# Small experts' scatter of the rows ahead moved to mid-panel, and TensorE's variants of the expert in another order

## The reference, cut to what matters

```python
def swiglu(h, w1, w3, w2):
    return (jax.nn.silu(h @ w1) * (h @ w3)) @ w2

def expert_block(args):           # within moe_swiglu
    toks, e = args
    xb = xf[toks]
    return (jax.nn.silu(xb @ w1[e]) * (xb @ w3[e])) @ w2[e]
...
y = jnp.zeros((n_tok, d), jnp.float32).at[row_tok].add(out.reshape(n_rows, d).astype(jnp.float32) * row_w[:, None])
```

## Time and profile before

| | us |
|---|---|
| median of 3 runs | 1699.87 (1699.73 to 1705.61) |
| the profiled execution, device time | 1696.55 |
| its span, first to last instruction | 1694.7 |
| TensorE busy | 1528.6 (90%) |
| VectorE busy | 762.5 (45%) |
| ScalarE busy | 510.7 (30%) |
| DMA, mean over the span | 296 GB/s |

### The profile page before, as it was taken

One profiled execution on the slowest core, in us unless ns is written; L12 is line 12 of the kernel. 1 busy time (PEld: TensorE's weight loads), 2 busy tenths in 40 slices (PEclk: granted clock), 3 DMA queues, 4 the chain that ended last, 5 costly groups with the idle time before them and its releaser, 6 DMA issues.

```text
span 1694.7 us, 22256 instructions
## 1 busy us (share of the span) xinstructions
PE 1528.6 (90%) x8462; PEld 1069.9 (63%) x8463; DVE 762.5 (45%) x851; ACT 510.7 (30%) x531; POOL 36.7 (2%) x40
## 2 busy tenths in 40 slices
PE   5999999999999999778999879999787978999974
PEld 2587767888587775334886339999543434788431
DVE  5696777775697675003884001000100100787104
ACT  1375425344275422003773000000100101775000
POOL 1200010000100000000000000000000000000000
PEclk9999999999999999999999999999899999999998
DMA  9885349874497532998998998777499999999994
GB/s 362 307 322 205 124 174 335 283 271 154 145 353 242 180 139 103 395 396 290 393 376 291 394 396 307 262 260 263 147 393 397 392 394 395 367 383 344 362 395 166
DMA packets 210536, 502.36 MB, mean 296 GB/s; under 512 B 9137, under 2 KB 13409, under 8 KB 210481
## 3 DMA queue, kind: packets, MB, share of 16 engines
q1 hardware_dynamic: 208770, 496.15, 80.4%
q0 software_dynamic: 1712, 5.43, 1.0%
HBM read 500.50 MB, written 1.05 MB: 296 GB/s over the span
## 4 chain that ended last, share of the span: by engine, by line
PE 69%; DMA 21%; DVE 5%; issue 2%; ACT 1%; SPq 1%; DVEq 0%; ACTq 0%
DMA w_raw<-in_exp_w_dram 20%; PE ps L1541 12%; PE ps L1542 11%; PE ps L1543 11%; PE ps L2246 6%; PE ps L2188 5%; PE ps L2178 4%; PE ps L1547 4%; PE ps L2256 3%; PE ps L2007 2%; PE ps L1981 2%; PE ps L2108 1%; DMA w_raw<-in_w_mod_mix_dram 1%; SPq L407 1%; DVE gates L1145 1%
## 5 line engine op out<-in xcount | busy, mean ns | idle before, releaser
L2178 PE MATMUL ps<-w_raw,x_rows 128*64 128x256 f32 x2240 | 270.0, 386 | 72.3 <-DMA w_raw<-in_exp_w_dram 60.2
L1541 PE MATMUL ps<-w_hi,actT_hi 128*128 128x512 f32 (+1 forms) x768 | 302.3, 394 | 11.8 <-ACT gates L680 3.5
L1543 PE MATMUL ps<-w_hi,actT_lo 128*128 128x512 f32 (+1 forms) x768 | 294.6, 384 | 0.0
L1542 PE MATMUL ps<-w_lo,actT_hi 128*128 128x512 f32 (+1 forms) x768 | 294.5, 383 | 0.0
L2178 PEld LDWEIGHTS ps<-w_raw,x_rows 128*64 128x64 f32 x2240 | 151.6, 137 | 192.3 <-DMA w_raw<-in_exp_w_dram 106.7
L928 DVE TENSOR_TENSOR w_lo<-w_raw,w_hi 128x2048 fp32r<-128x2048 f32 x78 | 178.5, 2289 | 92.9 <-ACT w_hi L515 92.7
L1443 DVE TENSOR_TENSOR gated<-silu,ps 128x256 f32<-128x256 f32 x35 | 14.7, 421 | 417.4 <-PE ps L2178 417.4
L515 ACT CAST w_hi<-w_raw 128x2048 fp32r<-128x2048 f32 x78 | 148.8, 1909 | 112.1 <-PE ps L1543 97.4
L1344 DVE TENSOR_TENSOR w_lo<-w_raw,w_hi 128x2048 fp32r<-128x2048 f32 x72 | 164.9, 2291 | 26.2 <-ACT w_hi L766 24.0
L1541 PEld LDWEIGHTS ps<-w_hi,actT_hi 128*128 128x128 f32 x768 | 145.8, 190 | 45.5 <-issue 11.9
L1543 PEld LDWEIGHTS ps<-w_hi,actT_lo 128*128 128x128 f32 x768 | 145.6, 190 | 28.8
(11 more groups left out here) (285 smaller groups left out, 1346.2 us busy)
## 6 DMA issues: line engine op xcount, KB each, us to landing
w_raw<-in_exp_w_dram SPq DMA_DIRECT2D x336, 1024.0 KB, 10.9
w_raw<-in_ffn_w_dram SPq DMA_DIRECT2D x33, 1024.0 KB, 5.2
w_raw<-in_w_mod_mix_dram SPq DMA_DIRECT2D x24, 1024.0 KB, 9.1
w_raw<-in_w_mod_ffn_dram SPq DMA_DIRECT2D x24, 1024.0 KB, 5.9
w_raw<-in_w_gate_dram SPq DMA_DIRECT2D x24, 1024.0 KB, 7.0
w_raw<-in_w_in_dram SPq DMA_DIRECT2D x14, 1024.0 KB, 6.6
w_raw<-in_w_out_dram SPq DMA_DIRECT2D x8, 1024.0 KB, 5.0
w_raw<-in_w_branch_c_dram SPq DMA_DIRECT2D x4, 1024.0 KB, 5.0
```

The lines of the kernel that those rows point to most:

```text
L1541: MM(to, hi, w_h, start=first, stop=False)
L1542: MM(to, hi, w_l, start=False, stop=False)
L1543: return MM(to, lo, w_h, start=False, stop=last)
L2178: ins = MM(half(to, c, HALF_N), x_few[:, k, :], w_raw[:, i % RING, at:at + HALF_N], start=k == 0, stop=k == KD - 1)
```

## The change

In the small variant the scatter of the expert ahead, the adds, the turn of the place, its copy and the next picks leave the first panel and stand behind the last piece of the third panel of the panel loop (`LATE`), in PSUM banks 1, 2, 3, 6 (`FEW_SUMS`) and 7 (`FEW_PLACE`), since bank 0 accumulates by then. Bank 0 is opened after a wait for the last expert's results to have been read out of it, and the wait for the new place stands behind the panel loop. DVE's panel loop ends a panel earlier, and the last panel is written out. The scatter of the other variants and the last one behind the loop keep their places; `scatter` waits in addition for the adds of the expert before. TensorE's variants stand in the order two-block, wide, split, small.

```diff
 HALF_N = BANK // 2
 WIDE = P + 16
 LOGITS = 4
+
+LATE = 3
+FEW_SUMS, FEW_PLACE = (1, 2, 3, 6), 7
 
 DVE_MIX_STEPS, DVE_DENSE_STEPS, DVE_ROUTE_STEPS = 39, 22, 32
 ACT_MIX_STEPS = 2
...
                     first_rows(1)
+                    act.sem_inc(y_act, 1)
...
                             act.sem_inc(split_hi, EXPERT.n_split)
                             act.sem_inc(part_hi_ready, 1)
                             gate_of(1, done0, panel_0)
-                            act.wait_ge(place_sent, e + 1)
-                            A(place[:, 0, :], ps[:, 0, 0:SEQ], ACT.Copy).then_inc(place_ready, 1)
                             with act.Fori(1, NP) as p:
                                 done, at = act.snap(done0 + (p - 1) * PANEL_PIECES), act.snap(panel_0 + p)
                                 gate_of(5, done, at)
                                 gT_part(at)
+                                with act.If(p == LATE):
+                                    act.wait_ge(place_sent, e + 1)
+                                    A(place[:, 0, :], ps[:, FEW_PLACE, 0:SEQ], ACT.Copy).then_inc(place_ready, 1)
                             gT_part(panel_0 + NP)
                             with act.If(e < EXPERTS - 1):
                                 first_rows(e + 2)
...
                         dve.wait_ge(gathered_lo[0], n)
                         nc.vector.tensor_copy(x_wide[:, 3:6, :], rows_bank(HW3 + 2)).then_inc(xg_lo_ready[0], 1)
 
-                    def add_rows(experts):
+                    def add_rows(experts, sums=range(4)):
                         for t in range(TT):
                             for c in range(2):
                                 dve.wait_ge(scattered, experts * 4 + (2 * t + c + 1))
                                 part = yacc[:, t, c * BANK:(c + 1) * BANK]
-                                TTn(part, part, bank(2 * t + c), ALU.add).then_inc(added, 1)
+                                TTn(part, part, bank(sums[2 * t + c]), ALU.add).then_inc(added, 1)
 
                     pick_tokens(0)
                     first_rows(1)
+                    dve.sem_inc(y_dve, 1)
                     dve.wait_ge(yacc_zero, 1)
                     with nc.Fori(0, EXPERTS, engines=[dve.engine], hint_back_edge=True, head_slot={dve.engine: 0}) as e:
                         count = dve.value_load(counts_i[0:1, bass.ds(e, 1)], min_val=0, max_val=SEQ)
...
                             dve.sem_inc(gT_lo_ready, NP)
                             dve.sem_inc(ahead_ready, SPLIT)
                             dve.sem_inc(part_lo_ready, 1)
-                            met(0, done0)
-                            met(1, done0)
-                            with dve.If(e > 0):
-                                add_rows(e)
-                            nc.vector.memset(hbuf[HALF_P:P, 0, :], 0.0)
-                            met(2, done0)
+                            for i in range(3):
+                                met(i, done0)
                             gate_of(3, done0, panel_0)
-                            pick_tokens(e + 1)
-                            with dve.Fori(1, NP) as p:
-                                done, at = dve.snap(done0 + (p - 1) * PANEL_PIECES), dve.snap(panel_0 + p)
+
+                            def panel(done, at):
+
                                 for i in (4, 5, 6):
                                     met(i, done)
                                 gate_of(7, done, at)
                                 for i in (8, 9):
                                     met(i, done)
+
+                            with dve.Fori(1, NP - 1) as p:
+                                panel(dve.snap(done0 + (p - 1) * PANEL_PIECES), dve.snap(panel_0 + p))
+                                with dve.If(p == LATE):
+                                    with dve.If(e > 0):
+                                        add_rows(e, FEW_SUMS)
+                                    nc.vector.memset(hbuf[HALF_P:P, 0, :], 0.0)
+                                    dve.wait_ge(place_sent, e + 1)
+                                    pick_tokens(e + 1)
+                            panel(dve.snap(done0 + (NP - 2) * PANEL_PIECES), panel_0 + (NP - 1))
                             done6 = dve.snap(done0 + (NP - 2) * PANEL_PIECES)
 
                             with dve.If(e < EXPERTS - 1):
...
                                     ins = MM(to, part[:, t, k * P:(k + 1) * P], pick[:, t, P:2 * P], start=t == 0, stop=t == 1)
                             ins.then_inc(signal, 1)
 
-                    def scatter(blocks, experts):
-                        pe.wait_ge(y_act, experts)
-                        pe.wait_ge(y_dve, experts)
+                    def scatter(blocks, experts, to):
+                        pe.wait_ge(added, experts * 4)
+                        pe.wait_ge(y_act, experts + 1)
+                        pe.wait_ge(y_dve, experts + 1)
                         for t in range(TT):
                             for c in range(2):
                                 for b in range(blocks):
-                                    ins = MM(bank(2 * t + c), place[:, b, t * P:(t + 1) * P], hbuf[:, b, c * BANK:(c + 1) * BANK],
+                                    ins = MM(bank(to[2 * t + c]), place[:, b, t * P:(t + 1) * P], hbuf[:, b, c * BANK:(c + 1) * BANK],
                                              start=b == 0, stop=b == blocks - 1)
                                 ins.then_inc(scattered, 1)
 
-                    def scatter_rows(experts):
+                    def scatter_rows(experts, to=range(4)):
                         rows_before = nc.snap(rows_reg, min_val=0, max_val=SEQ)
                         with pe.If(rows_before <= P):
-                            scatter(1, experts)
+                            scatter(1, experts, to)
                         with pe.Else():
-                            scatter(2, experts)
+                            scatter(2, experts, to)
 
                     pe.wait_ge(zeros_set, 1)
                     pe.wait_ge(pick_ready, 1)
...
                                     ins = TR(ps[:, HW1, c * P:(c + 1) * P], gated[0][:, c * P:(c + 1) * P], ident)
                                 ins.then_inc(gT_sent, 1)
 
-                            up_raw(0, "A", 0, loads0)
-                            up_raw(1, "A", 1, loads0)
-                            with pe.If(e > 0):
-                                scatter_rows(e)
-                            up_raw(2, "B", 0, loads0)
-                            pe.wait_ge(added, e * 4 + 4)
-                            for t in range(TT):
-                                ins = TR(ps[:, 0, t * P:(t + 1) * P], pick_w[:, t, 0:P], ident)
-                            ins.then_inc(place_sent, 1)
-                            up_raw(3, "B", 1, loads0)
-                            pe.wait_ge(place_ready, e + 1)
+                            for i, kind, h in ((0, "A", 0), (1, "A", 1), (2, "B", 0), (3, "B", 1)):
+                                up_raw(i, kind, h, loads0)
+                            pe.wait_ge(y_act, e + 1)
+                            pe.wait_ge(y_dve, e + 1)
                             MM(bank(0), zeros[:, 0:P], zeros[:, :], start=True, stop=False)
-                            with pe.Fori(1, NP) as p:
-                                loads, at = pe.snap(loads0 + (p - 1) * 16), pe.snap(panel_0 + p)
+
+                            def panel(loads, at):
+
                                 pe.wait_ge(silu_ready, at)
                                 up_raw(4, "A", 0, loads)
                                 up_raw(5, "A", 1, loads)
...
                                 pe.wait_ge(gT_hi_ready, at)
                                 down_raw(8, 0, loads)
                                 down_raw(9, 1, loads)
+
+                            with pe.Fori(1, NP) as p:
+                                panel(pe.snap(loads0 + (p - 1) * 16), pe.snap(panel_0 + p))
+                                with pe.If(p == LATE):
+                                    with pe.If(e > 0):
+                                        scatter_rows(e, FEW_SUMS)
+                                    for t in range(TT):
+                                        ins = TR(ps[:, FEW_PLACE, t * P:(t + 1) * P], pick_w[:, t, 0:P], ident)
+                                    ins.then_inc(place_sent, 1)
+                            pe.wait_ge(place_ready, e + 1)
                             turn(panel_0 + NP)
                             next_rows(1)
                             pe.wait_ge(gT_hi_ready, panel_0 + NP)
...
                                 ins = TR(ps[:, d // 4, d % 4 * P:(d % 4 + 1) * P], yT_whole[:, d, :], ident)
                             ins.then_inc(y_turned, 1)
 
-                        with pe.If(count <= P):
+                        with pe.If(count > WIDE):
+                            gather_second()
+                            expert(2)
+                        with pe.Else():
```

(15 more changed lines are left out.)

## The result

| | before | changed |
|---|---|---|
| median, us | 1702.74 (1699.73 to 1705.86, 4 runs) | 1782.80 (1780.46 to 1785.75, 4 runs) |
| ratio to before | | 1.0485, 95% interval 1.0459 to 1.0511 |
| profiled execution, us | 1696.55 | 1782.34 |
| its span, us | 1694.7 | 1780.4 |

The account below looks back on a forecast made before the run. Bound: weights' DMA in small experts, TensorE in the wide one, both full in split ones (engines taken). Scatter -8, code loads +56.6 and cold clock +9.8 made +58.4 us, forecast median 1758, range 1690 to 1785.

Parts of the forecast that it names:

- the sum of the gaps: TensorE's waits for code at the starts of the eight experts, each entry paying for its far jumps: +56.6 us.
- E5's term: Start of a small expert after a small one: six landed pieces wait for TensorE, which catches up; 0, at most +6 us.
- the price of a load: TensorE's fetch of code not held: 3.1 us with the weights' DMA idle, 5.3 with it full.
- the loop's end before E2 and E7: Jump to the loop's end before two small experts: paid as before at the first, 1.3 us added at the second.
- E4's term: Start of the small expert after the wide one: two more loads at 3.1 us, +6.2.
- E0: First expert in the loop, a small one: its entry pays three loads at 3.1 us, +9.3.
- E6: Seventh expert in the loop, a split one: its entry pays two loads at 5.3 us, +10.6.
- The scatter, -8: Scatter moved to mid-panel in small experts: saves DMA idle time at their starts, -8 us, bounds 0 and -15.4.
- The cold clock, +9.8: First pieces run slower behind new long gaps before four experts: 1.95, 2.9, 2.9 and 1.95 us.
- Rival 1: TensorE keeps the loop's code held, only the first expert's loads are paid: -8.4 us, 1691; chance 0.24.
- Rival 3: Mid-panel scatter in small experts becomes a DVE wait delaying slot releases: +12 us, 1712 if alone; chance 0.04.
- The rule of the Trainium skill's page: Only two code lines held, so jumps back to the loop's head cost some 22 us more, about 1780; weighed, not adopted.

Follow-up runs that it names:

- order alone: Kernel before with TensorE's variants in the order of the change, the scatter left where it was: 1791.69 us, ratio 1.0527 to before.
- scatter alone: Changed kernel with TensorE's dispatch put back as before (small variant first), so only the scatter moves to mid-panel: 1689.05 us, ratio 0.9937 to before.
- the kernel without the two-block code: Changed kernel minus TensorE's code for the two-block variant, never run on this input; variant order otherwise kept, small one last: 1686.33 us, ratio 0.9912 to before.
- wide last: Kernel before with the mid-panel scatter and the two large variants swapped in memory (small, split, two-block, wide): 1686.13 us, ratio 0.9942 to before.
- Large first, then small and split: Mid-panel scatter, memory order two-block, wide, small, split, compare for the large ones at the loop's head: 1702.79 us, ratio 1.0039 to before.

## Why the prediction was right and wrong

The forecast was slower by 58 us, by code fetched again at every entry, in a range of 1690 to 1785; measured were 1782.80 and 82 us by the ratio. The mechanism is the one forecast: the run with the order alone has the whole loss and its gaps, the run with the scatter alone has a gain. The step that failed is the sum of the gaps, put at +56.6 us: they measured +83.8, or 78.6 after what E5 won back. Three of its parts were too low, namely E5's term (0, with 10.1 left of 15.3), the price of a load (3.1, where a jump took 4.25 to 4.6) and the loop's end before E2 and E7 (1.3, where a fourth jump was paid in full). E4's term erred the other way, by 10.8, so that part of the nearness of 1758 to 1783 is luck. Gaps in detail, forecast and measured in the two profiles:

| entry | forecast | measured |
|---|---|---|
| E0 | +9.3 | 13.49 - 0.72 = +12.8 |
| E1 | +5.3 | 12.68 - 5.29 = +7.4 |
| E2 | +9.3 | 17.78 - 1.26 = +16.5 |
| E3 | +5.3 | +5.5 |
| E4 | +6.2 | 4.81 - 9.41 = -4.6 |
| E5 | 0 | +15.3, of which 10.1 stayed |
| E6 | +10.6 | +12.7 |
| E7 | +10.6 | +18.3 |

- **The price of a load, 3.1 us, was too low.** I divided E4's gap of 9.41 by its three packets. A jump is what is paid, not a packet: with the DMA idle 4.25 us each at E0, and the dispatch of the change makes three of them. With the DMA full one jump took 4.9 to 5.5 us (4.92, 5.20, 5.41 and 5.47 above), as forecast for E3; the two before E1 and E6 took 12.68 and 12.65, 6.3 each where 5.3 was forecast.
- **E2 and E7** are reached from the split variant, which no longer runs into the loop's end: by the order of the code four jumps to code not held stand in a row (to the end, the second compare, the third, the small variant), 17.78 and 18.33, 4.4 to 4.6 each. I counted three and 1.3 for the end, because that was its visible remnant at E2 before.
- **E4 had the wrong sign.** After the wide expert I had all of the small one's way loaded again. By the order of the code the head and the compares had just been used by the wide expert or stand next to it, so that only the small variant's own packets were missing. The gap of 4.81 us, the price of one jump, fits that.
- **E5's zero was wrong**, the largest single error of reasoning. I let six landed pieces wait for TensorE. A stage bound by bytes has no store of landed pieces: E4's last ones were used as they came, and behind them only those already asked for could arrive. The strip above shows what that is worth: the DMA is full for some 9 us of the gap of 15.32 and empty for some 10, and E5, which takes 106.6 us after its gap where it took 111.8 before (start to start less the gap at E6, 119.2 - 12.65), wins back 5.2; in the run with the scatter alone, where E5 has no gap, it takes 111.8 as before. The rest, 10.1, is lost.
- **The scatter, -8**, measured -10.7 (7.5 to 13.8) alone and some -7 by the ratios of the change and the order alone. By stretch of the two profiles E4 gave 4.6 (forecast 4.2), E7 1.7 (1.5), and E2 0.5 in place of 2.2, for which no run gives the reason. No cost of the mid-panel place shows.
- **The cold clock, +9.8**: outside the gaps the stretches of the changed kernel differ from before by +1.1 (E0), -0.9, +1.3, +4.8, -4.6, -5.2, +1.4 and +1.1 (E7), start to start and less the gap that ends each. E4 and E5 hold the scatter's gain and the catching up; the others sum to +8.7 with the scatter's gains at E2 and E7 in them. The size came near in part by luck: E3, the wide expert, has 4.8 where 2.9 was forecast, and E2, E6 and E7 have 1.3, 1.4 and 1.1 for 1.95, 2.9 and 1.95.

The sum of it: +83.8 of gaps, -1.2 of stretches, and 3.2 us by which E0's rows were ready later (668.60 against 665.39), 85.8, and the span grew by 85.7.

Rival 1, that the code stays held, fell at the point named for it: q8 is not silent over E5. But it holds two packets away, in the kernel without the two-block code. Rival 3, a wait in mid-panel, did not show: in E2 DVE's four adds stand at 1006.1 to 1008.6, some 53 us behind the start (forecast 45), and the strip of that stretch is full. The rule of the Trainium skill's page "Runtime: NRT & Kernel Launch", section "Instruction fetch mechanics", that a taken branch out of two held lines forces a fetch, would have given about 1780. Its time was near; its reason is not this kernel's: in the kernel without the two-block code E6 and E7 start with no gap after jumps over several packets, and no code packet moves from 1320 to 1655.

## What to carry to other kernels

In a loop with variants chosen at run time, count the code packets (some 250 instructions each) that a pass touches: the head, every compare of the dispatch, the variant, the loop's end, and what other passes between touch. While all of it was held, as without the two-block code, jumps left no gap; in the changed kernel they were paid again in each pass, 4 to 6 us each, and a stage bound by transfers stood still too. Such a count was too coarse to foretell every gap here. So keep the compares of the dispatch together at the head, leave the frequent variant behind it as the kernel before does, and look at the code queue's packets in the profile before and after such a move.

## What the runs showed of the hardware

- TensorE keeps several packets of code, by estimate some six to eight: without the two-block code six packets were fetched from 640 to 700 us, and E0, E1 and E2 then ran to 1020 with none; with the dispatch of the change eight were fetched in E5's stretch alone, right behind E4, an expert of the same variant.
- Code that never runs costs time by standing between code that does: the two-block variant is never entered here, and without it the time is some 11 us lower with the small variant first (ratio 0.9872 against 0.9937) and some 97 lower with it last (0.9912 against 1.0485), where one far jump to the small variant goes with it.
- The wide expert is slower behind a gap of 5 us: less the gap at its end it took 181.2 us in the five kernels without a gap before it, and in the other five 2.3 (order alone) to 4.8 us more (the change; 2.7 with wide last). The stretch table of the changed kernel (columns as in the earlier trace rows) has a granted clock of 0.98 in it, where the same 174 us from the expert's start, 1019 to 1193, had 1.00 before:

```profile
1066.00:1240.00 174.00, 172.68 (x1360) 170.42 (x1361) 10.72 (x17) 7.38 (x11) 0.00 (x0) 0.98 0.76 252
```

- Large first, then small and split gave a spread of 27 us between executions (22 without the longest), where the others stay within 11. What decides which packet is dropped was not found.
